# State-space inputs of steps 4 to 6 between the input product's last two tiles, of step 7 ahead of the first output half

## The reference

```
b_bar = ((lam_bar - 1.0) / lam)[..., None] * lax.complex(b_re, b_im)
bu = jnp.einsum('bcgi,gpi->bcgp', u_c, b_bar);  bu[:, 0] += lam_bar * state
_, states = lax.associative_scan(combine, (a_elem, bu), axis=1)   # s = lam_bar * s + bu
y = jnp.einsum('bcgp,gip->bcgi', states, c_mat).real
y = y + d_skip * u;  z = gelu(y);  out = z * sigmoid(z @ w_glu + b_glu)
```

## Time and profile before

| | us |
|---|---|
| median of 3 runs without profile | 4006.46 (4006.16 to 4007.76) |
| the profiled execution | 4015.36 |
| its span, first to last instruction | 4014.0 |
| TensorE busy | 3801.4 |
| VectorE, ScalarE, GpSimd busy | 2571.7, 1798.8, 1483.2 |
| mean granted TensorE clock | 0.976 of full |

### The profile page before, as it was taken

The page is one execution under the profiler, slowest core; times in us unless marked ns, Lnnn a source line. Parts: engine busy times, 40 slices in busy tenths (PEclk is TensorE's granted clock), DMA queues, the critical chain, the costliest instruction groups (busy, mean ns, idle before and its releaser), DMA issues.

```text
span 4014.0 us, 64390 instructions
## 1 busy us (share of the span) xinstructions
PE 3801.4 (95%) x27340; PEld 3235.3 (81%) x27340; DVE 2571.7 (64%) x3636; ACT 1798.8 (45%) x2801; POOL 1483.2 (37%) x726
## 2 busy tenths in 40 slices
PE   6898999998998999989899999999989999999998
PEld 3786888787877887888778888888878878888887
DVE  0435743785358897668879676876566876445457
ACT  1435343644345444445544444444445554333334
POOL 0332343233322441004344444444544434444443
PEclk8999999999999999999999999999789999999999
DMA  9653665354643453005346565656345435455553
GB/s 392 270 228 147 239 254 205 155 192 173 239 168 116 178 182 125 23 16 219 143 174 222 198 241 189 223 223 266 129 171 202 174 129 192 184 189 189 189 188 127
DMA packets 61231, 748.64 MB, mean 187 GB/s; under 512 B 7040, under 2 KB 9216, under 8 KB 17552
## 3 DMA queue, kind: packets, MB, share of 16 engines
q1 hardware_dynamic: 49536, 696.74, 45.8%
q0 software_dynamic: 9344, 45.69, 3.0%
q10 hardware_dynamic: 2064, 2.10, 0.1%
HBM read 727.65 MB, written 16.84 MB: 185 GB/s over the span
## 4 chain that ended last, share of the span: by engine, by line
PE 78%; DVE 12%; ACT 5%; DMA 2%; issue 1%; POOL 1%; SPq 0%; another core or an unknown queue 0%; DVEq 0%; ACTq 0%; POOLq 0%
PE ps L369 44%; PE ps L370 22%; DVE pieces L322 2%; DMA ring<-in_ada 2%; PE ps L2228 2%; ACT pieces L306 2%; PE ps L789 2%; PE ps L3594 1%; DVE r L1172 1%; PE ps L1898 1%; DVE opa L570 1%; DVE scr L591 1%; PE ps L1043 1%; ACT scr L674 1%; PE ps L643 0%
## 5 line engine op out<-in xcount | busy, mean ns | idle before, releaser
L369 PE MATMUL ps<-opa,pieces 128*128 128x512 f32 x6192 | 2251.8, 406 | 53.4 <-DVE pieces L322 35.8
L340 POOL TENSOR_TENSOR pieces<-ring,pieces 128x1024 fp32r<-128x1024 f32 x539 | 1343.5, 2493 | 2181.9 <-ACT pieces L306 2166.6
L370 PE MATMUL ps<-opa,pieces 128*128 128x256 f32 x6192 | 1740.2, 281 | 0.0
L306 ACT ACTIVATE pieces<-ring 128x1024 fp32r<-128x1024 f32 (+1 forms) x1110 | 1098.4, 1036 | 812.9 <-PE ps L370 810.8
L369 PEld LDWEIGHTS ps<-opa,pieces 128*128 128x128 f32 x6192 | 1170.9, 189 | 349.4 <-issue 31.6
L370 PEld LDWEIGHTS ps<-opa,pieces 128*128 128x128 f32 x6192 | 1177.2, 190 | 8.9 <-issue 5.3
L369 PE MATMUL ps<-opb,pieces 128*128 128x512 f32 x2560 | 909.5, 397 | 18.7 <-DVE pieces L322 13.2
L322 DVE TENSOR_TENSOR pieces<-ring,pieces 128x1024 fp32r<-128x1024 f32 (+1 forms) x571 | 722.4, 1265 | 271.0 <-ACT pieces L306 267.5
L370 PE MATMUL ps<-opb,pieces 128*128 128x256 f32 x2560 | 725.5, 283 | 0.0
L369 PEld LDWEIGHTS ps<-opb,pieces 128*128 128x128 f32 x2560 | 482.9, 189 | 140.4 <-issue 15.2
L370 PEld LDWEIGHTS ps<-opb,pieces 128*128 128x128 f32 x2560 | 483.7, 189 | 0.1
(11 more groups left out here) (432 smaller groups left out, 3348.5 us busy)
## 6 DMA issues: line engine op xcount, KB each, us to landing
ring<-in_up SPq DMA_DIRECT2D x64, 2048.0 KB, 7.7
ring<-in_down SPq DMA_DIRECT2D x64, 2048.0 KB, 7.7
ring<-in_win SPq DMA_DIRECT2D x56, 2048.0 KB, 7.5
ring<-in_ada SPq DMA_DIRECT2D x48, 2048.0 KB, 12.0
ring<-in_wout SPq DMA_DIRECT2D x24, 2048.0 KB, 7.6
ring<-in_evin SPq DMA_DIRECT2D x18, 2048.0 KB, 7.8
ring<-in_evout SPq DMA_DIRECT2D x8, 2048.0 KB, 7.8
ring<-in_xkv SPq DMA_DIRECT2D x8, 2048.0 KB, 7.7
```

What stands on the lines that cost most here:

```text
L306: a.do.activation(K.parts_of(p)[0][:, s, :], w[:, s, :], ACT.Copy).then_inc(*K.hi.up((p, h)))
L340: g.do.tensor_tensor(lo[:, s, :], w[:, s, :], hi[:, s, :].bitcast(F), ALU.subtract).then_inc(*K.lo2.up(p))
L369: pe.do.matmul(b[:, 0:512], hi[:, k, :], op[:, 512 * k:512 * k + 512], start=i == 0, stop=False)
L370: t = pe.do.matmul(b[:, 0:256], lo[:, k, :], half(op, 0, k), start=False, stop=i == kt - 1)
```

## The change

Steps 4 to 6 get their inputs after tile 14 and ahead of tile 15, in rounds of three row groups over all four powers; step 7 gets its own after tile 15 and ahead of the first output half, in rounds of one. Tile 15 takes the bank of tile 14, and step 7 later that same bank. VectorE draws two half steps at tile 13 (before 1), three at tile 14 (before 2) and three ahead of the reduce of tile 15 (before two behind it). The input tables go to `u5` and `mixw` by turns, the output tables to tile 14's slot, tile 15's slot, `u5` and tile 15's slot. The third output table is asked for when steps 8 to 11 have their inputs. ScalarE's feed of the first gate tile waits for output half (0, 1) where it waited for the inputs of step 15.

```diff
@@ -1625,7 +1625,9 @@
     f = K.place("s5", q, 16384)
     rot = lambda a, x, n, w: [a[:, x + w * i:x + w * i + w] for i in range(n)]
     z = (K.first["odin"] + 14) % 2 * 4096
-    K.TC, K.TB = [K.mixw, f[:, 4096 - z:8192 - z]], [u5[:, 4096:8192], f[:, z:z + 4096]]
+    K.KC = K.mixw
+    K.TB = [u5[:, 4096:8192], K.mixw]
+    K.TC = [f[:, z:z + 4096], f[:, 4096 - z:8192 - z], u5[:, 4096:8192], f[:, 4096 - z:8192 - z]]
     K.an5 = rot(u5, 8192, 2, 512)
     K.K5, K.aq, K.at5 = K.scr[:, 0:1536], K.scr[:, 1536:2048], K.scr[:, 2048:2560]
     K.sq5, K.wv5 = rot(K.scr, 2560, 2, 256), rot(K.scr, 3072, 2, 512)
@@ -3364,24 +3366,18 @@
 
 
 def load_c(K, e, s):
-    e.do.dma_start(K.TC[s % 2], K.D["s5tc"][s]).then_inc(*K.load["tc%d" % (s % 2)].up(("tc", s), 16))
+    e.do.dma_start(K.TC[s], K.D["s5tc"][s]).then_inc(*K.load["tc%d" % s].up(("tc", s), 16))
 
 
 def load_b(K, e, s):
-    to, done = K.TB[0], K.load["tb%d" % s]
+    to, done = K.TB[s % 2], K.load["tb%d" % s]
     e.do.dma_start(to[:, 0:1024], K.D["s5b"][s]).then_inc(*done.up(("tb", s), 16))
     e.do.dma_start(to[:, 1024:4096], K.D["s5tb"][s]).then_inc(*done.up(("tb", s), 16))
 
 
-def load_powers(K, e, s):
-    for k in range(3, -1, -1):
-        src = K.D["s5tb"][s][:, 1024 * k - 1024:1024 * k] if k else K.D["s5b"][s]
-        e.do.dma_start(K.TB[1][:, 1024 * k:1024 * k + 1024], src).then_inc(*K.load["pw%d" % k].up(("tb", s, k), 16))
-
-
 def load_k(K, e, s):
 
-    e.do.dma_start(K.TC[0], K.D["s5tc"][s]).then_inc(*K.load["kc"].up(("kc", s), 16))
+    e.do.dma_start(K.KC, K.D["s5tc"][s]).then_inc(*K.load["kc"].up(("kc", s), 16))
     e.do.dma_start(K.BT5[s % 2], K.D["s5bt"][s]).then_inc(*K.load["bt%d" % (s % 2)].up(("bt", s), 16))
 
 
@@ -3418,16 +3414,18 @@
 
     sp, p = K.sp, K.first["odin"]
     kept_all(K, sp)
+    sp.wait_ge(*K.prod.of(("K", 0)))
+    load_b(K, sp, 1)
+    sp.wait_ge(*K.prod.of(("z5", 3)))
+    load_b(K, sp, 2)
     sp.wait_ge(*K.tile.of(p + 14))
-    load_powers(K, sp, 1)
+    load_c(K, sp, 0)
     sp.wait_ge(*K.tile.of(p + 15))
     load_c(K, sp, 1)
-    sp.wait_ge(*K.prod.of(("z5", 3)))
-    load_b(K, sp, 2)
-    sp.wait_ge(*K.prod.of(("y5", 3)))
+    sp.wait_ge(*K.prod.of(("z5", 7)))
+    load_b(K, sp, 3)
+    sp.wait_ge(*K.prod.of(("z5", 11)))
     load_c(K, sp, 2)
-    sp.wait_ge(*K.prod.of(("z5", 7)))
-    load_powers(K, sp, 3)
     sp.wait_ge(*K.prod.of(("y5", 7)))
     load_c(K, sp, 3)
 
@@ -3442,10 +3440,14 @@
         if n in ORDER_K:
             pe_s5_direct(K, ORDER_K[n])
         if n == 12:
-            last = [K.bank["tile", K.first["odin"] + t] for t in (10, 11, 12)]
-            K.z5b = K.ps[3:8] + last + K.ps[4:8] + last + K.ps[4:5]
+            a, b, c = (K.bank["tile", K.first["odin"] + t] for t in (10, 11, 12))
+            K.z5b = K.ps[3:8] + [a, c, b] + K.ps[4:8] + [a, c, b] + K.ps[4:5]
             K.pe.wait_ge(*K.act.of(("K", 0)))
-            pe_s5_in(K, 0)
+            pe_s5_in(K, 0, (0, 1, 2, 3))
+        if n == 14:
+            K.pe.wait_ge(*K.dve.of(("u", 13)))
+            pe_s5_in(K, 1, (0, 1, 2))
+            K.tb.i += 2
 
 
 def pe_s5_direct(K, s):
@@ -3456,7 +3458,7 @@
     pe.wait_ge(*was)
     pe.wait_ge(*K.load["kc"].of(("kc", s)))
     pe.wait_ge(*K.act.of(("bt", s)))
-    C = K.TC[0].rearrange("p (k j c i) -> p k j c i", k=4, j=16, c=2)
+    C = K.KC.rearrange("p (k j c i) -> p k j c i", k=4, j=16, c=2)
     B = K.BT5[s % 2].rearrange("p (c j i) -> p c j i", c=2, j=16)
     for m in range(4):
         for c in range(2):
@@ -3493,8 +3495,10 @@
         if n == 0:
             dve_rstd(K, ("nm", 1), K.rstd)
             v.wait_ge(*K.dve.now())
+        for _ in range(3 * (n == 15)):
+            next(steps)
         dve_normed_by_fours(K, p + n, K.U[:, n, :], K.rstd, ("us", n)).then_inc(*K.dve.up(("u", n)))
-        for _ in range(min(n - 12, 2)):
+        for _ in range({13: 2, 14: 3}.get(n, 0)):
             next(steps)
     drain(steps)
 
@@ -3558,42 +3562,36 @@
 
 
 def pe_s5(K):
-    pe_s5_in(K, 1)
+    K.pe.wait_ge(*K.dve.of(("u", 15)))
+    pe_s5_in(K, 1, (3,))
     pe_s5_out(K, 0, 0)
-    pe_s5_in(K, 2)
+    pe_s5_in(K, 2, (0, 1, 2, 3))
     pe_s5_out(K, 0, 1)
-    pe_s5_in(K, 3)
+    pe_s5_in(K, 3, (0, 1, 2, 3))
     for s in range(1, 4):
         pe_s5_out(K, s, 0)
         pe_s5_out(K, s, 1)
 
 
-def pe_s5_in(K, s):
+def pe_s5_in(K, s, rows):
 
     pe = K.pe
     bs = K.z5b[4 * s:4 * s + 4]
-    K.bank.update({("z5", 4 * s + q): bs[q] for q in range(4)})
-    pe.wait_ge(*K.dve.of(("u", 4 * s + 3) if s == 0 else ("u", 14)))
+    K.bank.update({("z5", 4 * s + q): bs[q] for q in rows})
     if s >= 2:
+        pe.wait_ge(*K.dve.of(("u", 4 * s + 3)))
         pe.wait_ge(*K.dve.of(("p", 4 * s - 4)))
         pe.wait_ge(*K.act.of(("w", 4 * s - 4)))
-    if s % 2 == 0:
-        pe.wait_ge(*K.load["tb%d" % s].of(("tb", s)))
+    pe.wait_ge(*K.load["tb%d" % s].of(("tb", s)))
     B = K.TB[s % 2].rearrange("p (k m c t) -> p k m c t", k=4, m=4, c=2)
-    rounds = [((0, 1), (0, 1, 2)), ((0, 1), (3,)), ((2, 3), (0, 1, 2, 3))] if s == 1 else [((0, 1, 2, 3), (0, 1, 2, 3))]
-    for powers, rows in rounds:
-        if s == 1 and 3 in rows:
-            pe.wait_ge(*K.dve.of(("u", 15)))
-        for r in powers:
-            if s % 2:
-                pe.wait_ge(*K.load["pw%d" % (3 - r)].of(("tb", s, 3 - r)))
-            for m in range(4):
-                for c in range(2):
-                    for q in rows:
-                        q0 = 32 * q
-                        t = pe.do.matmul(bs[q][:, 256 * c + 64 * m:256 * c + 64 * m + 64], B[q0:q0 + 32, 3 - r, m, c, :],
-                                         K.U[q0:q0 + 32, 4 * s + m, 64 * r:64 * r + 64], start=r + m + c == 0, stop=r + m + c == 7)
-    t.then_inc(*K.prod.up(("z5", 4 * s + 3)))
+    for r in range(4):
+        for m in range(4):
+            for c in range(2):
+                for q in rows:
+                    q0 = 32 * q
+                    t = pe.do.matmul(bs[q][:, 256 * c + 64 * m:256 * c + 64 * m + 64], B[q0:q0 + 32, 3 - r, m, c, :],
+                                     K.U[q0:q0 + 32, 4 * s + m, 64 * r:64 * r + 64], start=r + m + c == 0, stop=r + m + c == 7)
+    t.then_inc(*K.prod.up(("z5", 4 * s + rows[-1])))
 
 
 Y5_AT = {(1, 1): 5, (2, 1): 6, (3, 1): 5}
@@ -3608,9 +3606,8 @@
     pe.wait_ge(*K.act.of(("w", {(1, 1): 9, (2, 1): 10}.get((s, h), 0))))
     if (s, h) in Y5_AFTER:
         pe.wait_ge(*K.dve.of(("u5", Y5_AFTER[s, h])))
-    if s:
-        pe.wait_ge(*K.load["tc%d" % (s % 2)].of(("tc", s)))
-    C = K.TC[s % 2].rearrange("p (k j c i) -> p k j c i", k=4, j=16, c=2)
+    pe.wait_ge(*K.load["tc%d" % s].of(("tc", s)))
+    C = K.TC[s].rearrange("p (k j c i) -> p k j c i", k=4, j=16, c=2)
     direct = K.K5.rearrange("p (m k i) -> p m k i", m=16, k=3)
     y = r3(b[:, 0:512], 2)
     for m in (2 * h, 2 * h + 1):
@@ -3638,7 +3635,7 @@
         act_s5_tables(K, n)
         if n % 2 and n < 15:
             act_s5_whole(K, n // 2 + 1)
-    a.wait_ge(*K.prod.of(("z5", 15)))
+    a.wait_ge(*K.prod.of(("y5", 3)))
     act_feed(K, K.first["glu"])
     act_s5_rows(K, 13)
     act_s5_gelu(K, 0, 4)
@@ -3696,7 +3693,7 @@
         if n < 16:
             c, b, M = K.cs5[n % 4], K.bank["z5", n][:, 0:512], K.m5[n % 2]
             over = lambda a: a[:, None, :].broadcast_to([P, 2, 256])
-            v.wait_ge(*K.prod.of(("z5", n // 4 * 4 + 3)))
+            v.wait_ge(*K.prod.of(("z5", 6 if 4 <= n < 7 else n // 4 * 4 + 3)))
             v.wait_ge(*K.act.of(("tab", n)))
             v.do.tensor_tensor(r3(M, 2), r3(b, 2), over(c[:, 256:512]), ALU.mult).then_inc(*K.dve.up(("m2", n)))
         if 0 <= n - 2:
```

More of the change, by code:

```diff
@@ L106, in __init__ @@
                                                  "auxb1", "auxb2", "fw", "dsac", "sf", "rwkc", "rwkc2", "lora", "s5b", "s5c",
-                                                 "io5", "mem", "kc", "lamT", "row5", "bt0", "bt1", "tc0", "tc1", "tb0", "tb2", "pw0", "pw1", "pw2", "pw3")}
+                                                 "io5", "mem", "kc", "lamT", "row5", "bt0", "bt1", "tc0", "tc1", "tc2", "tc3", "tb0", "tb1", "tb2", "tb3")}
         self.kept = [sem(f"table{i}_stored") for i in range(2)]
```

## The result

The changed kernel takes 4014.94 us (median of 13 runs, 4006.58 to 4021.44) where the kernel before took 4006.46 beside it (13 runs, 4004.83 to 4012.56). The ratio is 1.0021, 95% interval 1.0012 to 1.0029. A second set of runs gave 4016.56 (12) against 4011.48 (24), ratio 1.0006, interval 0.9996 to 1.0016. So the change costs between nothing and 0.3%. Forecast were 3997.5 us and a range that ended at 4005.5: outside, on the wrong side.

The account below looks back on a forecast made before the run. TensorE bounds the kernel (78% of the chain of waits). Last inputs end at 2923.9 against 2933.87, tail unchanged: 10.0 us gained, 1 taken off; 9.0 off the 4006.46 median gives 3997.5 us, range 3992.5 to 4005.5.

Parts of the forecast that it names:

- the transfers: Table loads on SyncE's queue: three DMA issues fewer and one 2 MB transfer more, costed at nothing.
- nothing on an engine's path moves: Stretch up to the end of tile 14: no change expected, so three row groups start at 2858.6.
- The inputs of steps 8 to 11: Block after the first output half: starts at the higher clock, 7.37 us instead of 13.86, to 2901.4.
- The tail: From the end of the last inputs to the last outputs: 34.4 us as before, ending at 2958.3 for 2968.26.
- Three row groups: Between tiles 14 and 15, inputs of steps 4 to 6: clock falls 4.4 us in, 9.5 us, to 2868.1.
- lone row group: Step 7's inputs, ahead of the first output half: 64 rounds, clock falls 1.5 us in, 12.3 us, to 2889.0.
- first output half: After step 7's inputs: runs without a gap, clock back after 3.3 us, 5.0 us in all, to 2894.0.
- Rival B: Clock does not come back in the first output half: gain of 2.1 us, 4004.4 us; chance 0.15.
- E's wait: Wait for the tables stays, the new transfer order being held up on SyncE: nothing gained, 4006 us; chance 0.02.
- C's turning point: Slower, 4010.6 us, chance 0.08; with no output-half rise, loss where step 7's inputs end later than 2891.1.
- A: Clock holds through the three row groups between tiles 14 and 15: gain of 12.9 less 1, 3994.6 us; chance 0.22.
- D: No clock fall while TensorE has work, lone group 7.1 us: gain of 20, 3986.5 us; chance 0.03.

Follow-up runs that it names:

- before: The kernel without the change, traced six times: stretch from the first inputs to the second gate tile 126.6 to 135.5 us, mean 131.2; median 4006.46 us.
- e1: Changed kernel with table transfers moved out of the blocks of small products (steps 0 to 3, steps 8 to 11): 4005.99 us, ratio 0.9999 to the kernel before.
- e3: Changed kernel with inputs of steps 4 to 7 made together after tile 15 and transfers moved off the small products: 4000.62 us, ratio 0.9972 to the kernel before.
- e5: Changed kernel with transfers moved off the small products, except that the input tables of steps 12 to 15 leave as in the changed kernel: 4011.69 us, ratio 1.0002.
- e6: Changed kernel, inputs of steps 4 to 7 joined after tile 15, first transfers moved, last input tables leaving with step 7's inputs: 4000.08 us, ratio 0.9969 to the kernel before.
- after_5: The changed kernel, unedited, fifth trace: 4012.16 us.
- _3: The changed kernel, unedited, third trace: 4018.41 us.
- e2: Changed kernel with the inputs of steps 4 to 7 made together, four row groups to a round, after tile 15, its tables kept: 4010.63 us, ratio 0.9996.
- e4: Kernel before plus one 2 MB transfer, output table 0 reloaded in place beside the inputs of steps 0 to 3: 4015.72 us, ratio 1.0008.
- after: The changed kernel, first trace: profiled execution 4016.31 us; median of 13 runs 4014.94 us, ratio 1.0021 to the kernel before.
- _4: The changed kernel, unedited, timed again on another chip against the kernel before: 4016.56 us, ratio 1.0006.
- after_again: The changed kernel, unedited, second trace: 4015.79 us.

## Why the prediction was wrong, point by point

**Step that failed first: the transfers.** "Three DMA issues fewer and one transfer of 2 MB more, on queues with nothing else to carry: I cost them at nothing". The queue on SyncE had nothing else to carry; the DMA engines had. What is read above as TensorE's own instructions comes over them, 16 KB at a time. In windows of 0.4 us the start of that packet can be read for every trace. In the ten undisturbed first blocks (six of before, e1, e3, e5, e6) it starts 2.6 to 2.9 us into the block, ahead of record 222 at 6.47 us. Beside a table transfer it starts late, and the stop grows with it:

| block, in the order of the packet's start | the window with the packet's start opens, us into the block | stop, us |
|---|---|---|
| first: ten undisturbed | 2.6 to 2.9 | 0 |
| first: after_5, _3, e2, e4, after, _4, _again | 5.1, 5.1, 5.3, 5.4, 5.5, 5.8, 6.1 | 1.21, 1.44, 1.21, 1.56, 1.44, 1.90, 2.03 |
| third: six of before, e2, e3, e4 | -0.7 or earlier | 0 |
| third: e1, e6 | -0.3, -0.3 | 0 |
| third: after_again, after, _5, _3, _4, e5 | 0.3, 1.2, 1.2, 1.3, 1.4, 1.9 | 0.55, 1.41, 1.36, 1.44, 1.49, 1.74 |

All 13 stops end 2.3 to 2.8 us after the opening of the packet's window. So in an undisturbed first block the packet starts at 2.7, work could go on some 2.5 later, and TensorE has enough until 6.47: a slack of 1.3 us. In after a packet 2.8 us late should leave a stop of 1.5; it was 1.44. That the transfer is the cause is shown by rows on both sides and by adding and removing it. The clock belongs to the same cost: in 12 of the 13 blocks with a stop it had fallen 2.1 us after the stop's end or sooner, and in the ten first blocks without one it held. From the start of the first block to the end of tile 14, e1 and e5 take 18.8 us each and the five traces of after 21.7 to 24.2. The Trainium skill, "Runtime: NRT & Kernel Launch", section "Instruction fetch mechanics", says that instructions are streamed in 16 KiB blocks over a DMA queue of the engine's own and that the cost of crossing a block is mostly hidden. The block's size agrees with the trace (a packet of 0.02 MB, as the view rounds it); "mostly hidden" holds in before's input blocks and not beside a 2 MB transfer, where it cost 0.6 to 2.0 us.

The trace that the forecast was made from had such stops already, in the output halves behind the last inputs. Here are two of them in its timeline of TensorE, then a window ahead of each (columns as in the windows of after above):

```profile
2950.95 2.14 PE L3620 MATMUL ps<-s5u,scr 32*32 32x128 f32 x38 [2.65 <-issue]
...
2967.88 0.32 PE L3629 MATMUL ps<-s 128*32 128x64 f32 x7 [0.35 <-issue]
```

```profile
2945.60:2948.60 3.00, 2.70 (x150) 2.17 (x138) 3.00 (x7) 2.43 (x4) 0.67 (x1) 1.00 0.99 426
...
2962.60:2965.50 2.90, 2.90 (x103) 2.44 (x95) 1.46 (x4) 0.81 (x2) 0.00 (x0) 0.68 0.00 0
```

The longer comes beside a table transfer (426 GB/s), and its packet starts in 2948.40 to 2948.80, the opening 2.6 us before work goes on; all six traces of before have one of 1.3 to 2.9 us there. So the sign of this price stood in the forecast's own base. The shorter has no transfer beside it, so a full DMA is not the only way to such a stop. In none of the 17 traces do two packets start less than 3.2 us apart; that products which use up their instructions faster than that outrun them is a reading of this, which no run tests.

**What this did to the terms.** Up to the end of tile 14, "nothing on an engine's path moves": 18.9 us had been read from tile 12's end, after took 22.0 (2841.3 to 2863.3), since half a tile ran at half clock behind the stop: 3.1 us. The inputs of steps 8 to 11, sized 7.37, took 12.1 (2899.7 to 2911.8) with stop and fall: 4.7 us. The tail was 35.3 against 34.4: 0.9; after's chain has two short stops in it (0.37 and 1.64 us, neither beside a transfer) where before's has one of 0.35. Together 8.7 of the 10.0 us that the path gained before 1 us was taken off; most of the rest is the small misses named below. e1, without the transfers, gives the first two back (18.8 us to the end of tile 14, 7.8 for the inputs of steps 8 to 11).

**Steps that held.** Three row groups 9.60 for 9.5; from tile 14's end to the end of step 7's inputs 31.0 for 30.4; lone row group 11.71 for 12.3; first output half 5.4 for 5.0, with the clock back at about 2898.6 (the sum's 0.86 of the state part should be 5/6, which changes under 0.1 us); 8.7 for 8.6 to the copy of step 8; 13.93 as said. Rival B's mechanism (no rise in the output half) did not occur, nor E's wait; the lone group ended 3.1 us past C's turning point of 2891.1, but late only because tile 14 was. A and D fell with the clock's loss at about 2867.9 and 2885.0, TensorE busy throughout. By the rule on idle gaps that the prediction cited there from the Trainium skill ("TensorE: Matmul & The Clock Gate", HAM oscillation) the lone group would have kept the clock. The trace disagrees again: it was lost 2.5 us into the lone group, and 4.6 us into the three row groups, which had no gap ahead of them.

**Second failure, the base.** The sum started from one trace of before and took its 13.86 us for what that kernel does. It does that in three traces of six; in the others they take 7.3 to 8.2 us already, and the stretch is 7.9 us shorter (127.3 for 135.2). Subtracting from the base's median a gain that the base has half the time counts half of it twice. Against before's mean stretch, e1's trace gains 6.2 us and not 9.9; its ratio of 0.9999 says even less.

**What was worth something.** The split itself was costed rightly and was still a bad trade: 21.3 us for products that take 8.1 in one piece where the clock holds (e2), and 11.5 and 12.3 where it falls (e3, e6). With quiet tables, joining them takes the stretch from 125.0 to 121.1 us and the ratio from 0.9999 to 0.9972 (each against before in its own rounds). The prediction had read that a round costs 0.111 us however many row groups are in it, and did not ask whether to split at all.

**Open.** The first comparison says 8 us of loss, the second 2 to 5, the traces 2.9; which is nearest can't be told against the noise of the untouched part. Why before sometimes gets the clock back around the first output half and sometimes not was not found, nor why four row groups in one block keep it in e2 and lose it in e3 and e6. That the 16 KB packets waited in the DMA engines, and not in what asks for them, is not shown.

## What to carry to other kernels

TensorE's instructions share the DMA engines with your data. A stretch of many tiny instructions (here 36 products and as many weight loads per us) needs new ones so often that a transfer of 2 MB beside it can stop TensorE; put bulk transfers beside large products or pauses. Before you call a transfer free, look for "issue" in the timeline of the kernel before and for the instruction queue in the DMA view. Where a round costs the same for one row group as for four, keep the groups together. And take several traces of the base before you subtract from one: a step that is long in one may be short in the next.

## What was not expected of the hardware

- TensorE stood 0.55 to 2.03 us without a wait, in every execution of after behind the same two records, and went on 2.3 to 2.8 us after the opening of the window in which its 16 KB instruction packet began; in the first block the packet began 2.4 to 3.4 us late beside a table transfer (399 to 430 GB/s in after).
- The kernel before has two forms 7.9 us apart over the same instructions, by whether the granted clock is back at 2.4 GHz by the start of one block of small products or 1.7 us into it (7.3 to 8.2 us long), or not (13.9).
- TensorE also stood with no transfer beside it, 0.35 us in before and 1.64 in after, the window with the start of an instruction packet opening some 2.5 us earlier.
- The clock was 1.00 when the first stop of after began and fell some 2 us after its end; behind the stop of 0.55 us in after_again it did not fall.
- Four row groups held 2.4 GHz for 7.37 us in before, but in e6 they lost it at about 2866.7, 2 us into the joined block (12.32 us in all), and in e3 as well (11.54), where e2 kept it for 8.1.
